# Attention probabilities of chunks 2 to 9: through DRAM scratch and a VectorE block transpose instead of TensorE transposes

## What is computed

```python
def _window_attention(q, k, v, q_gain, k_gain, sink, rel_bias):
    ...
    s = einsum('bnqhgd,bnkhd->bnhgqk', qb, kw) * (HEAD_DIM ** -0.5)
    s = where(valid, s + bias, -inf)        # 128 queries x up to 384 keys
    m = maximum(max(s, axis=-1), sink)
    p = exp(s - m)
    denom = sum(p, axis=-1) + exp(sink - m)
    o = einsum('bnhgqk,bnkhd->bnqhgd', p / denom, vw)
```

## Time and profile before

| | |
|---|---|
| timed runs | 2319.92, 2317.18, 2318.82 us, median 2318.82 |
| profiled execution, its time | 2318.55 us |
| its span, first to last instruction | 2317.1 us |
| mean granted TensorE clock, share of full speed | 0.995 |
| PE busy | 2273.0 us (98%) |
| DVE busy | 1239.2 us (53%) |
| ACT busy | 622.8 us (27%) |
| POOL busy | 542.8 us (23%) |
| output stretch of layer 0 / layer 1 | about 543 to 721 us / 1695 to 1873 us |

### The profile page before, as it was taken

How to read it: one execution, slowest core, us unless ns; L and a number is a source line. 1 busy time by engine, 2 the same in 40 slices (tenths; PEclk the granted TensorE clock), 3 DMA queues, 4 the chain that set the end, 5 groups by cost and what they waited for, 6 DMA issues and landing times.

```text
span 2317.1 us, 33010 instructions
## 1 busy us (share of the span) xinstructions
PE 2273.0 (98%) x12766; PEld 1613.8 (70%) x12766; DVE 1239.2 (53%) x2399; ACT 622.8 (27%) x1445; POOL 542.8 (23%) x552
## 2 busy tenths in 40 slices
PE   8999999999999999999999999999999999999998
PEld 6556587874556778887775665878755567888776
DVE  3554466586647344555236434765865463455542
ACT  3221233464332111111132212335633421111111
POOL 1003454144211111111110034532432111111111
PEclk9999999999999999999999999999999999999999
DMA  4002132221127988878530111312212279888883
GB/s 155 21 25 68 55 122 74 74 91 56 74 73 254 348 302 292 299 264 284 148 120 21 37 55 59 119 60 82 83 55 82 82 274 343 300 290 274 284 295 83
DMA packets 149653, 352.16 MB, mean 152 GB/s; under 512 B 9941, under 2 KB 38105, under 8 KB 149498
## 3 DMA queue, kind: packets, MB, share of 16 engines
q1 hardware_dynamic: 134234, 308.11, 37.1%
q0 software_dynamic: 15264, 41.95, 7.4%
HBM read 307.75 MB, written 42.28 MB: 151 GB/s over the span
## 4 chain that ended last, share of the span: by engine, by line
PE 93%; DVE 4%; DMA 1%; ACT 1%; issue 1%; POOL 0%; SPq 0%; DVEq 0%; ACTq 0%; POOLq 0%
PE ps L1842 89%; PE ps L2127 1%; PE ps L2188 1%; DVE HT L1784 1%; PE ps L1861 1%; DVE TMP L1248 1%; DMA HT<-h_sample,idxs 0%; PE ps L1894 0%; DVE HT L1248 0%; PE ps L2139 0%; DVE TMP L1257 0%; ACT SCR L1051 0%; DMA MID<-w_in 0%; DVE SCR L1248 0%; POOL SCR L753 0%
## 5 line engine op out<-in xcount | busy, mean ns | idle before, releaser
L1842 PE MATMUL ps<-MID,HT 128*128 128x512 f32 (+3 forms) x2560 | 694.2, 491 | 4.8 <-DMA MID<-w_in 3.0
L1842 PEld LDWEIGHTS ps<-HT,MID 128*128 128x128 f32 x4096 | 557.2, 191 | 16.4 <-issue 15.4
L1842 PE MATMUL ps<-HT,MID 128*128 128x160 f32 (+1 forms) x4096 | 560.5, 299 | 1.0 <-DVE HT L1248 0.9
L1842 PEld LDWEIGHTS ps<-MID,HT 128*128 128x128 f32 (+1 forms) x2560 | 293.7, 157 | 248.3 <-issue 207.7
L1842 PE MATMUL ps<-RING,HT 128*128 128x256 f32 (+2 forms) x1760 | 395.8, 392 | 1.7 <-DVE RING L1252 1.3
L1842 PEld LDWEIGHTS ps<-RING,HT 128*128 128x128 f32 (+1 forms) x1760 | 310.7, 189 | 83.5 <-issue 40.7
L1842 PE MATMUL ps<-HT,RING 128*128 128x512 f32 (+1 forms) x960 | 350.0, 522 | 0.0
L1842 PEld LDWEIGHTS ps<-HT,RING 128*128 128x128 f32 x960 | 180.2, 190 | 157.8 <-issue 149.8
L1784 DVE STREAM_TRANSPOSE HT<-HT 32x256 f32<-32x256 f32 x576 | 251.0, 436 | 18.3
L1257 DVE SCALAR_TENSOR_TENSOR HT<-HT,ps 128x160 f32<-128x160 f32 (+1 forms) x128 | 40.9, 319 | 397.1 <-ACT HT L1210 395.1
L850 POOL DMA_INDIRECT y_prompt<-SCR,idxp x32 | 50.5, 1578 | 583.1 <-ACT SCR L1220 562.2
(11 more groups left out here) (268 smaller groups left out, 2177.2 us busy)
## 6 DMA issues: line engine op xcount, KB each, us to landing
MID<-w_gate SPq DMA_DIRECT2D x32, 2048.0 KB, 9.4
MID<-w_up SPq DMA_DIRECT2D x32, 2048.0 KB, 15.0
MID<-w_down SPq DMA_DIRECT2D x32, 2048.0 KB, 16.2
RING<-w_in SPq DMA_DIRECT2D x20, 1024.0 KB, 5.3
SCR<-cs_rows SPq DMA_DIRECT2D x20, 1024.0 KB, 5.2
MID<-w_out SPq DMA_DIRECT2D x8, 1024.0 KB, 6.4
y_sample<-RING SPq DMA_DIRECT2D x16, 512.0 KB, 2.6
h_sample<-HT SPq DMA_DIRECT2D x16, 512.0 KB, 2.6
```

The source lines that it names most:

```text
L1842: return pe.matmul(out, a, b, start=start, stop=stop)
```

## The change

Chunks n = 0 and n = 1 keep the TensorE transposes. For n = 2 to 9 the way of the probabilities becomes:

1. `bia` and `PSC` are laid out as 4 quadrants of 32 keys (`b`), heads, then up to 3 blocks of 32 (`x`), so that the scores of PE read the keys in that order. DVE's `attn_shift` and ACT's `attn_exps` use patterns of four pieces; for n < 2 DVE's addition is split in two instructions, one for each head.
2. `attn_scale` on POOL is four instructions, one for each quadrant, instead of one.
3. SP's new `move_p(n)` waits for `pn_made` (and for `turn_p(n - 1)` of DVE from n = 3 on), stores `PSC` (768 KB as laid out in SBUF) to scratch in DRAM, waits for that store, and issues four loads, each to the 32 partitions of one quadrant of `PB`. It is called for n = 3 to 9 ahead of the store of x of chunk n - 2, and for n = 2 after the store of h2 of chunk 0.
4. DVE's new `turn_p(n + 1)` waits for the four loads and for `o_made(n)`, and turns `PB` in blocks of 32x32 to `PT`: one instruction on 128 x 1536 elements for `nk` = 3, four of 128 x 256 for `nk` = 2. It stands between `keep_h2(n - 1, 1)` and `keep_y(n + 1, 1)`, and in the hand-ordered iteration n = 8 between `route(7)` and `rounds`.
5. PE's `turn_p` and ACT's `keep_p` for n = 2 to 9 are gone.
6. In layer 0 the bias goes by a staging tile and four POOL copies. In both layers the loads of two parts of `w_out` come after the rows of mLSTM chunks 6 and 7 instead of 3 and 4.

```diff
+        prr = nc.dram_tensor("p_rows", (2 * P, AH * 384), F32, kind="Internal").ap()
...
+        PSCF = [SCR[:, 1536 * b:1536 * (b + 1)] for b in range(2)]
+        PSC = [a.rearrange("p (b h x) -> p b h x", b=4, h=AH) for a in PSCF]
+        PBF = HT[:, 8704:8704 + 4 * AH * 96]
+        PB = PBF.rearrange("p (a h x) -> p a h x", a=4, h=AH)
...
                     for c in range(NC):
                         m_load(c)
-                        if c in (3, 4):
-                            k = 2 * c - 4
+                        if layer == 0 and c == 2:
+                            sp.wait_ge(hot_loaded, 32)
+                            sp.wait_ge(wk_made, 2 * len(STEPS))
+                            sp.dma_start(STAGE, bass.AP(tensor=btab.tensor, ...)).then_inc(hot_loaded, 16)
+                        if c in (6, 7):
+                            ...
+                            k = 2 * c - 10
                             sp.dma_start(WO[k], wo_rows[:, k:k + 2]).then_inc(wo_loaded, 16)
...
+                    def move_p(n):
+
+                        sp.wait_ge(pn_made, n + 1)
+                        if n >= 3:
+                            sp.wait_ge(p_turned, 2 * AH + n - 2)
+                        rows = prr[P * (n % 2):P * (n % 2) + P, :]
+                        sp.dma_start(rows, PSCF[n % 2]).then_inc(scratch_stored, 16)
+                        sp.wait_ge(scratch_stored, 16 + 16 * (n - 1))
+                        for b in range(4):
+                            sp.dma_start(PBF[32 * b:32 * b + 32, :].rearrange("p (a x) -> p a x", a=4),
+                                         rows[:, 384 * b:384 * (b + 1)].rearrange("(a j) x -> j a x", a=4)).then_inc(scratch_loaded, 16)
+
                     for c in range(NC):
                         if c == NC - 2:
                             sp.wait_ge(o_made, NC)
                             gate_up_load(0)
+                        if 1 <= c and c + 2 < NC:
+                            move_p(c + 2)
                         sp.wait_ge(op_added, 2 * c + 2)
                         sp.dma_start(x_rows(ORDER[c]), XO[c % 2]).then_inc(x_stored[c % 2], 16)
                         sp.wait_ge(n2_scaled, c + 1)
                         sp.dma_start(h2_rows(ORDER[c]), H2[c % 2]).then_inc(h2_stored[c % 2], 16)
+                        if c == 0:
+                            move_p(2)
...
                     def attn_scale(n):
...
+                        v = PSC[n % 2][:, :, :, 0:w]
+                        for b in range(4):
+                            link(pool.tensor_tensor(v[:, b], v[:, b], ADEN[n % 2].unsqueeze(2).to_broadcast([P, AH, w]), ALU.mult),
+                                 pn_made if b == 3 else pool_chain, wait=b == 3)
...
+                        if layer == 0 and c == 3:
+                            pool.wait_ge(hot_loaded, 48)
+                            for h in range(AH):
+                                link(pool.tensor_copy(bia[:, h]..., STAGE[:, h]...))
...
-                        keep_p(n + 1)
+                        if n == 0:
+                            keep_p(1)
...
+                    def turn_p(n):
+
+                        nk, c0 = attn_keys(ORDER[n])
+                        dve.wait_ge(scratch_loaded, 64 * (n - 1))
+                        dve.wait_ge(o_made, n)
+                        out = PT.rearrange("p (h k a j) -> p a h k j", h=AH, k=3, a=4)[:, :, :, 0:nk, :]
+                        if nk == 3:
+                            link(dve.transpose(out.rearrange("p a h k j -> p a (h k) j"), PB.rearrange("p a h (k i) -> p a (h k) i", k=3)), p_turned)
+                            return
+                        for a in range(4):
+                            turned = link(dve.transpose(out[:, a], PB[:, a, :, 0:32 * nk]...), p_turned if a == 3 else dve_chain, wait=a == 3)
...
                         take_x(n)
                         keep_h2(n - 1, 1)
+                        turn_p(n + 1)
                         keep_y(n + 1, 1)
...
                     route_shift(n - 1)
                     route(n - 1)
+                    turn_p(n + 1)
                     dve.wait_ge(aff_turned, 1)
                     rounds(0, 15)
...
+                            keys = KT[64 * g:64 * g + 64, c0 * P:(c0 + nk) * P]
+                            if n >= 2:
+                                keys = keys.rearrange("p (k b i) -> p b k i", b=4, i=32)
...
-                            pe.wait_ge(p_kept, AH * (n + 1))
+                            if n < 2:
+                                pe.wait_ge(p_kept, AH * (n + 1))
+                            else:
+                                pe.wait_ge(p_turned, 2 * AH + n - 1)
...
-                        if n + 1 < NC:
-                            turn_p(n + 1, 0)
-                        out_proj(n, 0, 3, 4)
-                        if n + 1 < NC:
-                            turn_p(n + 1, 1)
-                        out_proj(n, 0, 4, 5)
+                        out_proj(n, 0, 3, 5)
```

More of the change, by code:

```diff
@@ L212, in program @@
         PT = VO[:, 0:AH * 384]
-        PSC = [SCR[:, 1536 * b:1536 * (b + 1)].rearrange("p (h k) -> p h k", h=AH) for b in range(2)]
+        PSCF = [SCR[:, 1536 * b:1536 * (b + 1)] for b in range(2)]
+        PSC = [a.rearrange("p (b h x) -> p b h x", b=4, h=AH) for a in PSCF]
+        PSN = [a.rearrange("p (h k) -> p h k", h=AH) for a in PSCF]
+        PBF = HT[:, 8704:8704 + 4 * AH * 96]
+        PB = PBF.rearrange("p (a h x) -> p a h x", a=4, h=AH)
+        STAGE = MID[:, bc_at:bc_at + AH * 384].rearrange("p (h k) -> p h k", h=AH)
         ident, tri = cstt[:, 0:P], [cstt[:, P:2 * P], cstt[:, 2 * P:3 * P]]
         ones1 = cstt[:, 3 * P:3 * P + 1]
-        bia = bias[:, :].rearrange("p (h k) -> p h k", h=AH)
+        bia = bias[:, :].rearrange("p (h b x) -> p h b x", h=AH, b=4)
         EW = [MID[:, j * 12288:(j + 1) * 12288] for j in range(2)]
@@ L1560, in attn_shift @@
                         if n >= 2 and j == 0:
[L1561 to L1562 removed]
+                            if n < 4:
+                                dve.wait_ge(p_turned, AH * (n - 1))
+                            else:
+                                dve.wait_ge(scratch_stored, 16 + 16 * (n - 3))
                         b = 6 if (n, j) == (0, 1) else 4
[L1564 to L1565 removed]
+                        if n < 2:
+                            v = PSN[n][:, j:AH:2, 0:nk * P]
+                            for q in range(2):
+                                h = j + 2 * q
+                                link(dve.tensor_tensor(PSN[n][:, h, 0:nk * P].rearrange("p (k b i) -> p b k i", b=4, i=32),
+                                                       ps[:, b + q, 0:nk * P].rearrange("p (k b i) -> p b k i", b=4, i=32),
+                                                       bia[:, h, :, at:at + w].rearrange("p b (k i) -> p b k i", i=32), ALU.add),
+                                     s_read if q else dve_chain)
+                        else:
+                            v = PSC[n % 2][:, :, j:AH:2, 0:w].rearrange("p b h x -> p h b x")
+                            tt(v, ps[:, b:b + 2, 0:nk * P].rearrange("p h (b x) -> p h b x", b=4), bia[:, j:AH:2, :, at:at + w], ALU.add, s_read)
+                        link(dve.tensor_reduce(out=m[:, j:AH:2], in_=v, axis=mybir.AxisListType.XY if n >= 2 else AX, op=ALU.max))
                         if j == 1:
@@ L1568, in attn_shift @@
                             tt(e, pr("sink"), neg, ALU.add, s_shift)
+                    def turn_p(n):
[5 more added lines that the diff above has]
+                            link(dve.transpose(out.rearrange("p a h k j -> p a (h k) j"), PB.rearrange("p a h (k i) -> p a (h k) i", k=3)), p_turned)
+                            return
+                        for a in range(4):
+                            turned = link(dve.transpose(out[:, a], PB[:, a, :, 0:32 * nk].rearrange("p h (k i) -> p h k i", k=nk)),
+                                          p_turned if a == 3 else dve_chain, wait=a == 3)
                     def attn_den(n):
@@ L2126, in turn_p @@
                         for b in range(nk):
-                            last = pe.transpose(ps[:, 6 + h % 2, b * P:(b + 1) * P], PSC[n % 2][:, h, b * P:(b + 1) * P], ident)
+                            last = pe.transpose(ps[:, 6 + h % 2, b * P:(b + 1) * P], PSN[n][:, h, b * P:(b + 1) * P], ident)
                         last.then_inc(p_turned, 1)
@@ L2300, in _ @@
                     out_proj(n, 0, 4, 5)
[L2301 to L2304 removed]
+                    out_proj(n, 0, 5, 7)
                     turn_y(n + 1, 0)
```

51 lines of the change are left out of this document (19 added, 32 removed).

## The result

The changed kernel takes 2332.45 us (median of 4 runs, 2330.81 to 2334.95), the kernel before 2318.53 (4 runs beside them): ratio 1.0061, 95% interval 1.0043 to 1.0078. It is 13.9 us slower. The forecast of 2333.0 holds, and so does its sign. The profiled execution took 2334.95 us with a span of 2333.5, 16.4 more than the span before; it is 2.5 us above its own median, so that differences against its rows come out that much larger than differences of medians.

A forecast was written before the change was run, and what follows sets the result against it. PE was taken to bound the kernel, busy 98% of the span, with DVE having only 1.04 us to spare; 3.8 + 2.2 + 0.2 + 1.0 = 7.2 us a layer, +14.4 on 2318.55, gave 2333, range 2318 to 2350.

The forecast's parts named there:

- its sign: Whole kernel: the change makes it slower, given a chance of 0.77, against 0.14 for within 0.2% and 0.09 for faster.
- prelude and round trip of n = 1: PE's products of chunk 2 wait for the first trip through DRAM: +3.8 us a layer, ends 2.2 and 6.8.
- clock behind it: After PE idles about 7 us in n = 1, the clock falls to 0.50: +2.2 us a layer, ends 0 and 3.2.
- iterations n = 2 to 7: PE's saved transposes against its waits for DVE's longer chain: +0.2 us a layer over the six.
- n = 8: The block transpose of chunk 9 between route(7) and the rounds on DVE delays the critical rounds: +1.0 us a layer.
- The waits in DVE's chain: PE waits ahead of its attention products: 1.44 us in n = 2 to 4, 0.91 in 5, 0.95 in 6 and 7.
- cover holds: Rival, n = 2 to 7: DVE's chain has more slack, so PE's gains are kept; 2318.6 us, no change; chance 0.13.
- Hidden things: Later round trips (seven us to spare), bias by way of POOL, later w_out loads, patterns in four pieces: no cost.
- the prelude's split additions: DVE's additions for n = 0 and 1 split in two, three of four on the path: +0.55 us.
- Faster: Rival: the cover holds and the first round trip is over by 550; 2301.8 us; chance 0.09.
- slow loads: Rival: loads to 32 partitions run at a quarter of the rate, some 14 us instead of 4.7; 2379 us; chance 0.08.
- A dearer transpose: Rival: DVE's block transpose costs 2.62 us, by pieces, 4 us a layer more; 2341 us; chance 0.12.

The follow-up runs named there:

- e_act_h2: Changed kernel, but from n = 2 on ACT instead of DVE copies the second half of h2, keep_h2(n - 1, 1): 2327.13 us, 1.0038 of the kernel before.
- ten filling products: Changed kernel plus ten PE products of constants that nobody reads, ahead of chunk 2's attention products in n = 1: 2329.64 us, 1.0052 of the kernel before.
- the exchange of two statements: Changed kernel, but SP stores the probabilities of chunk 2 ahead of the h2 of chunk 0: 2325.84 us, 1.0032 of the kernel before.
- early transpose: Changed kernel, but from n = 2 on DVE's block transpose stands ahead of keep_h2(n - 1, 0): 2338.3 us, 1.0089 of the kernel before.
- the last experiment: Changed kernel, but chunks 2 and 9 with PE, two DVE copies on ACT and the transpose ahead of take_x(n): 2307.25 us, 0.9947 of the kernel before.

## Why the prediction was right

By its own terms, in us a layer:

| step | predicted | layer 0 | layer 1 |
|---|---|---|---|
| prelude and round trip of n = 1 | +3.8 | +6.2 | +4.4 |
| clock behind it | +2.2 | +2.25 | +2.25 |
| iterations n = 2 to 7 | +0.2 | -0.7 | -0.7 |
| n = 8 | +1.0 | +0.9 | +0.3 |
| sum | +7.2 | +8.6 | +6.2 |

Together 14.8 against 14.4. That this is so close is in part luck: the first trip cost 3.0 us more than predicted over both layers, and the iterations n = 2 to 8 cost 2.6 less. The rest of the 16.4 lies outside: 1.15 at the start, before the output stretch of layer 0; 1.7 between the layers, where the prediction had nothing; 1.3 less at the end. The 1.15 is scatter between executions as far as the profiles tell: the first attention products of layer 0 start at 527.11 here, and between 525.39 and 527.31 in the eight experiments, which are alike up to there.

**The waits in DVE's chain.** 1.36 against 1.44 in n = 2 to 4, 0.83 against 0.91 in n = 5: right to 0.08. Three small errors nearly cancel in it. The handover that I left out is 0.14 us (`keep_y` ends at 606.65, the products start at 606.79) and makes the wait longer. Against it, DVE's chain from `keep_h2(n - 1, 0)` to the end of `keep_y(n + 1, 1)` grew by 1.67 (7.91 after, 6.24 before), not by 1.82, since the next instruction starts 0.07 before the transpose ends and `keep_y` is a little shorter; and PE gained 0.59 in it, not 0.66. The block transpose took 1.78 us against 1.79, so the rows of 32 partitions did carry to 128. That the chain has no hole was the argument against *cover holds*; `e_act_h2`, in which exactly one copy left the chain and exactly its length left the wait, shows it. For n = 6 and 7 the step was mis-sized: four transposes of 256 columns take 1.43 us together (0.36 each in a row), not 1.83, so the waits are 0.48 instead of 0.95 and each of these turns gains 0.33 where I had it lose 0.08.

**The round trip.** Its place, its start (scale of 3.49 us against 3.5) and the queue in which it stands were right. The landing of the store was mis-sized: 6.11 and 4.18 us behind the h2 store, against 4.8. The loads took 5.83 to DVE's start in layer 0 against my 4.7. The error of 2.4 us in layer 0 is the largest of all, inside the 6.8 of the upper end. That the queue was to blame for a part of it I had, at 1.3 us; the exchange of two statements brings 3.5 us in layer 1 and 4.9 in layer 0: 2.53 for the issue and 2.84 for the landing, less 0.5 that its loads take longer (6.33 from their issue to the transpose at 553.08).

**The clock.** 2.25 against 2.2, from a row at another place of the same kernel. The turn of 21.54 under ten filling products shows that it is the clock. That the size is the same was not sure from that row, which stands behind a wait of 2.04 us: after the store went ahead, waits of 3.91 and 3.49 cost 2.42 and 1.65.

**n = 8** came out at 0.9 in layer 0 against 1.0, by two errors that cancel: the four transposes take 1.43 us, 0.40 less than in the sum, and they wait 0.39 for their loads, which the prediction had as hidden. In layer 1 they wait for no load, and the first round comes 13.63 us after the products of chunk 8 instead of 13.99; with the wait for the gathered rows of the experts (0.83 there against 1.06 before, 0.92 against 0.91 in layer 0) that makes the 0.3. So the term by itself was mis-sized: 0.6, not 1.0.

**Hidden things.** The later round trips are covered in n = 2 to 7, where no transpose waits for a load; that of chunk 9 in layer 0 was not, by 0.39 us. PE's scores take 0.92 us on 384 keys and 0.70 on 256 with the strided read as without it. The bias by way of POOL and the moved `w_out` loads show no cost that stands out from the scatter, but no run took them out one by one; the prelude's split additions cost 0.56 (predicted 0.55), by the stretch from 1351.93 to the first attention products of layer 1 at 1689.49, 337.56 us, against 337.00 before.

**The rivals.** *Faster* and *slow loads* are out: the first trip ended at 559, not by 550, and a quarter of the store's rate would have made the loads 14 us long, where they took 5.83. *A dearer transpose* is out by the 1.78. For the block transpose the Trainium skill (VectorE: DVE Perf Modes, "The three transpose paths") gives 311 ns for 128x128 on VectorE and 390 on TensorE, both in bf16. Here, in float32, twelve such pieces in one instruction take VectorE 1.78 us, 0.15 each, and PE needs 0.109 a piece in a row. Neither figure is the price of a piece in a row, and here TensorE is the cheaper of the two. The measurement decides.

## What to carry to other kernels

Work moved off the engine that bounds a kernel is worth its time only if the engine that takes it has a hole at that point of its own chain; read how much it has to spare between the row that sets its start and the row that waits for it, and move as much off as you put on. A round trip through DRAM cost nothing here where it had a whole turn of some 20 us for its 12, and was paid where a pipeline starts; there, keep the first unit on the old path. A store on which something waits goes ahead of those on which nothing does.

## What was not expected of the hardware

The same store of the probabilities landed in 3.27 us when it stood first in its queue, and in 4.18 or 6.11 us with a store of 512 KB issued 0.37 us ahead of it: 0.9 or 2.8 us more, for a store which took 2.6 in the kernel before. Over the six profiles with this order (the changed kernel and five experiments) the landing is 6.06 to 6.37 us in layer 0 every time; in layer 1 it is 4.17 or 4.18 four times and 5.94 and 6.30 once each. What decides between the two isn't shown.

The turn of the layers changed by itself. From PE's wait for y of the first chunk to a landmark behind the projections of the recurrence (1340.40 before, 1351.93 after) it is 182.3 us before and 184.1 after, though nothing was changed there. Timeline of PE, then windows, of the changed kernel, to set beside the earlier trace rows:

```profile
1167.86 1.06 PE L1921 MATMUL ps<-cstt,MID 128*128 128x128 f32 x8 [2.08 <-DMA MID<-y_prompt]
...
1179.91 1.37 PE L1921 MATMUL ps<-cstt,MID 128*128 128x128 f32 x8 [2.85 <-ACT MID L924]
```

```profile
1167.86:1169.86 2.00, 1.06 (x8) 0.82 (x8) 1.23 (x2) 1.43 (x3) 1.68 (x7) 1.00 1.13 236
1169.86:1171.86 2.00, 1.70 (x4) 1.31 (x5) 0.31 (x2) 0.76 (x2) 1.33 (x4) 0.62 0.87 120
...
1179.86:1181.86 2.00, 1.95 (x10) 1.80 (x11) 1.15 (x2) 1.91 (x4) 0.58 (x2) 0.68 1.03 420
1181.86:1183.86 2.00, 2.00 (x5) 1.36 (x5) 0.98 (x2) 1.15 (x3) 0.73 (x3) 0.50 1.04 422
```

Before, the clock was at 0.50 from the first of these waits on the earlier trace rows, and back up when PE stood at the second, for ACT: what was lost ahead of it was waited for anyhow. Here it falls later after the first wait, and a second time behind the longer wait for ACT, where nothing covers it. The ten profiles fall into three kinds:

| profiled execution of | clock between the two waits | wait for ACT, us | clock right behind it | the stretch, us |
|---|---|---|---|---|
| before; early transpose | 0.50 within 0.5 us | 1.92; 2.06 | 1.00 | 182.3; 182.5 |
| changed; ten products | 0.50 from 2.5 us on, then 1.00 | 2.85; 2.83 | 0.50 | 184.1; 184.1 |
| the six other experiments | 1.00 | 4.28 to 4.80 | 0.50 | 184.4 to 184.9 |

A row of the last kind, with chunk 2 on PE:

```profile
1171.37 1.97 PE L1920 MATMUL ps<-cstt,MID 128*128 128x128 f32 x8 [4.37 <-ACT MID L922]
```

PE's wait for ACT ends 11.8 to 12.3 us after its wait for y in all ten, whatever the clock did in between. So a clock lost ahead of it costs nothing, and one kept there makes the wait longer, behind which the clock is lost at a price of some 2 us. Nearly every version pays this in its profile, and the kernel before doesn't. What decides where the clock falls stays open: no run changed that place alone. It need not be a property of the version: of the 16 timed runs of the kernel before that stand beside the first experiments, two took 2315.6 and 2315.7 us at a mean granted clock of 0.997, the others 2317.0 to 2318.9 at 0.995 or 0.996; of the five of the last experiment, two took 2303.2 and 2303.6 at 0.997, three 2307.3 to 2307.4 at 0.995. No such run was profiled, so where they kept the clock isn't shown.

The Trainium skill (TensorE: Matmul & The Clock Gate, "Why this matters for your kernels") advises against idle gaps between bursts of products. The waits of 8.78 and 3.91 us, behind which the clock was at 0.50, agree. That a wait of 1.94 to 2.27 us at the turn of the layers is followed by the lower clock at once in one execution, later in another and not before the next wait in a third is more than it says.
